# Turning pages, window keys, selected keys and probabilities as two 64-row halves in a decoder step

## The reference

```python
x_n, x_f = nsa_block(...), fox_block(...)      # both on the same projections of x
mix = (sigmoid(ga) * (x_n @ w_a) + sigmoid(gb) * (x_f @ w_b)) @ w_out
x = layer_norm(ALPHA * x + mix)
f = (gelu(conv(x @ w_up)) * (x @ w_gate)) @ w_down
x = layer_norm(ALPHA * x + f);  x = x + sigmoid(x @ w_ple_gate) * (p_emb @ w_ple)
```

## Time and profile before

| what | value |
|---|---|
| time, median of 3 runs | 2362.68 (2359.55 to 2363.3) |
| profiled execution, its own time | 2361.97 |
| its span, first to last instruction | 2360.2 |
| TensorE busy, matmuls | 2310.0 (98%) |
| VectorE, GpSimd, ScalarE busy | 1214.4, 833.7, 547.6 |
| mean granted TensorE clock | 0.998 |
| DMA moved | 240.36 MB, mean 102 GB/s |
| request stage | from 677.6 to 932.3 in the span |

### The profile page before, as it was taken

The page is one execution under the profiler, slowest core; times in us unless marked ns, Lnnn a source line. Parts: engine busy times, 40 slices in busy tenths (PEclk is TensorE's granted clock), DMA queues, the critical chain, the costliest instruction groups (busy, mean ns, idle before and its releaser), DMA issues.

```text
span 2360.2 us, 32397 instructions
## 1 busy us (share of the span) xinstructions
PE 2310.0 (98%) x11863; PEld 1518.5 (64%) x11863; DVE 1214.4 (51%) x3023; ACT 547.6 (23%) x1300; POOL 833.7 (35%) x874
## 2 busy tenths in 40 slices
PE   8999999999989998999999999999999999999999
PEld 4454566666667776788884478888888874443343
DVE  4886627787853334324225873334433334239765
ACT  0000116787753332111112121111111100001131
POOL 0000005565651002666634534333333436203531
PEclk9999999999999999999999999999999999999999
DMA  5422821031078887222226111111111126434101
GB/s 184 115 76 77 291 84 64 2 112 33 2 217 237 242 237 235 79 85 81 82 71 172 42 41 55 37 37 54 37 36 37 54 89 211 149 135 152 56 18 58
DMA packets 185959, 240.36 MB, mean 102 GB/s; under 512 B 53435, under 2 KB 128833, under 8 KB 184265
## 3 DMA queue, kind: packets, MB, share of 16 engines
q1 hardware_dynamic: 181018, 218.99, 30.2%
q0 software_dynamic: 3616, 9.73, 1.2%
q10 hardware_dynamic: 1168, 9.58, 1.2%
HBM read 216.18 MB, written 37.99 MB: 108 GB/s over the span
## 4 chain that ended last, share of the span: by engine, by line
PE 57%; DVE 2%; ACT 1%; issue 0%; DVEq 0%; ACTq 0%
PE ps L2254 37%; PE ps L2418 11%; PE ps L2307 5%; PE ps L2475 2%; PE ps L2405 1%; DVE xT L152 1%; PE ps L2483 1%; ACT xT L2528 0%; PE ps L2311 0%; DVE arena L3006 0%; ACT arena L2625 0%; DVE stats L2680 0%; PE ps L2350 0%; DVE xT L1409 0%; DVE queries L3009 0%
## 5 line engine op out<-in xcount | busy, mean ns | idle before, releaser
L2254 PE MATMUL ps<-xT,arena 128*128 128x272 f32 x1920 | 472.7, 393 | 1.8 <-DVE arena L1411 1.8
L2254 PEld LDWEIGHTS ps<-xT,arena 128*128 128x128 f32 x1920 | 363.9, 190 | 77.4 <-DVE arena L1411 2.2
L2254 PE MATMUL ps<-queries,arena 128*128 128x272 f32 x1312 | 331.6, 393 | 2.0 <-PEq L1451 1.0
L2254 PEld LDWEIGHTS ps<-queries,arena 128*128 128x128 f32 x1312 | 249.0, 190 | 54.1 <-DVE queries L2821 1.4
L235 PE MATMUL ps<-arena,xT 128*128 128x512 f32 (+1 forms) x512 | 198.3, 550 | 1.9 <-DMA arena<-in_w_in 1.1
L235 PEld LDWEIGHTS ps<-arena,xT 128*128 128x128 f32 x512 | 97.9, 192 | 101.9 <-issue 93.5
L2254 PE MATMUL ps<-arena 128*128 128x272 f32 x576 | 147.7, 393 | 0.0
L979 ACT ACTIVATE arena<-arena 128x640 f32<-128x640 f32 (+10 forms) x208 | 136.8, 660 | 33.9 <-DVE arena L929 26.1
L2418 PE MATMUL ps<-arena 128*128 128x512 f32 x312 | 140.6, 599 | 0.0
L816 PE MATMUL ps<-arena,queries 64*128 64x512 f32 (+9 forms) x704 | 132.6, 442 | 3.6 <-DVE arena L929 2.6
L2418 PE MATMUL ps<-xT,arena 128*128 128x512 f32 x304 | 131.4, 592 | 0.0
(11 more groups left out here) (357 smaller groups left out, 3411.8 us busy)
## 6 DMA issues: line engine op xcount, KB each, us to landing
arena<-in_cache_fox_kv SPq DMA_DIRECT2D x72, 256.0 KB, 4.0
arena<-in_w_ffn_down SPq DMA_DIRECT2D x68, 256.0 KB, 3.7
arena<-in_w_in SPq DMA_DIRECT2D x16, 1024.0 KB, 5.3
xT<-in_w_ffn_down SPq DMA_DIRECT2D x64, 256.0 KB, 3.6
xT<-in_cache_fox_kv SPq DMA_DIRECT2D x56, 256.0 KB, 6.3
arena<-in_cache_nsa_kv SPq DMA_DIRECT2D x64, 192.0 KB, 8.3
arena<-in_w_ffn_up SPq DMA_DIRECT2D x11, 1024.0 KB, 5.4
arena<-in_w_ffn_gate SPq DMA_DIRECT2D x11, 1024.0 KB
```

The costliest lines, as they stand in the source:

```text
L2254: mm = pe.matmul(ps[:, first + BANK_OF[z], 0:PIECE], weight[:, j, :], moving[:, j, :], start=(j == 0 and z in (1, 6, 5, 7)), stop=(j == kk ...
```

## The change

A new helper `turn_sides` turns eight tiles at once. Each 128-row tile is taken as two halves: rows 0 to 63 go through the upper half of the array into one bank and rows 64 to 127 through the lower half into another. The two banks together hold what two banks held before, but divided by row half instead of by tile. Both are entered before the first half, and both are signalled by the last one (`then_inc(ring_filled, 2)`). This takes the place of `turn` for the FoX key pages, the selected keys, the window keys, and the probabilities p_slc and p_fox. ScalarE copies the first halves of all eight tiles, VectorE the second halves, each in strips of 64 columns. The selected keys are grouped by request instead of by half of the rows, and `slc_scores` waits for all four banks before its first matmul. The raw rows, p_cmp, p_win, the new-row probabilities and the outputs are turned as before.

```diff
         if now:
-            yield from ((n, f"slc{x}{'ab'[r]}", r) for x in range(2) for r in range(2))
+            yield from ((n, f"slc{r}{'ab'[side]}", side) for r in range(2) for side in range(2))
...
+            def turn_sides(n, name_a, name_b, tiles):
+                banks = (enter(n, name_a), enter(n, name_b))
+                for x, src in enumerate(tiles):
+                    for side in range(2):
+                        rows = slice(side * HD, (side + 1) * HD)
+                        mm = pe.transpose(ps[:, banks[side], x * HD:(x + 1) * HD], src[rows], keep.ident[rows, rows])
+                mm.then_inc(ring_filled, 2)
+
             def keys(n, p):
                 pe.wait_ge(k_in[p % 4], 32 * (2 * n + p // 4 + 1))
-                for r in range(2):
-                    b = enter(n, f"k{p}{'ab'[r]}")
-                    for c in range(4):
-                        mm = turn(b, c * P, P, at.pages[:, p % 4, r, c * P:(c + 1) * P])
-                    mm.then_inc(ring_filled, 1)
+                turn_sides(n, f"k{p}a", f"k{p}b", [at.pages[:, p % 4, r, c * P:(c + 1) * P] for r in range(2) for c in range(4)])
...
             def slc_turns(n):
-                for x in range(2):
-                    for r in range(2):
-                        b = enter(n, f"slc{x}{'ab'[r]}")
-                        for j in range(4):
-                            mm = turn(b, j * P, P, at.raw[:, r, 2 * x + j // 2, j % 2, 256:384])
-                        mm.then_inc(ring_filled, 1)
+                for r in range(2):
+                    turn_sides(n, f"slc{r}a", f"slc{r}b", [at.raw[:, r, j // 2, j % 2, 256:384] for j in range(8)])
...
                 pe.wait_ge(win_in, 32 * (n + 1))
-                for r in range(2):
-                    b = enter(n, f"win{'ab'[r]}")
-                    for j in range(4):
-                        mm = turn(b, j * P, P, at.win[:, r, j, 0:P])
-                    mm.then_inc(ring_filled, 1)
+                turn_sides(n, "wina", "winb", [at.win[:, r, j, 0:P] for r in range(2) for j in range(4)])
...
+                for r in range(2):
+                    consumed(n, f"slc{r}a")
+                    consumed(n, f"slc{r}b")
                 for x in range(2):
-                    consumed(n, f"slc{x}a")
-                    consumed(n, f"slc{x}b")
...
-                    prob_turns(m, "p_slc0", at.p_slc, range(4))
-                    prob_turns(m, "p_slc1", at.p_slc, range(4, 8))
+                    turn_sides(m, "p_slc0", "p_slc1", [at.p_slc[:, j * P:(j + 1) * P] for j in range(NPAGE)])
...
-                    prob_turns(n, "p_fox0", at.p_fox, range(4))
-                    prob_turns(n, "p_fox1", at.p_fox, range(4, 8))
+                    turn_sides(n, "p_fox0", "p_fox1", [at.p_fox[:, j * P:(j + 1) * P] for j in range(NPAGE)])
...
-                        save(n, f"k{p}a", at.kT[:, p % 2, 0], tiles(ring.bank(n, f"k{p}a"), 4))
+                        save(n, f"k{p}a", at.kT[:, p % 2].rearrange("p r c q -> p (r c) q")[:, :, 0:HD], sides(ring.bank(n, f"k{p}a")))
...
-                        save(n, f"k{p}b", at.kT[:, p % 2, 1], tiles(ring.bank(n, f"k{p}b"), 4))
+                        save(n, f"k{p}b", at.kT[:, p % 2].rearrange("p r c q -> p (r c) q")[:, :, HD:P], sides(ring.bank(n, f"k{p}b")))
```

More of the change, by code:

```diff
@@ L1857, in exps, with sides @@
                                      accum_out=at.sums[:, j:j + 1]).then_inc(done, 1)
-            def tiles(b, m):
-                return ps[:, b, 0:m * P].rearrange("p (t q) -> p t q", t=m)
+            def sides(b):
+                return ps[:, b, :].rearrange("p (t q) -> p t q", t=8)
             def raw_rows(n, kv, par):
@@ L1893, in _ @@
                 if late:
-                    save(m, "p_slc0", at.pT_slc[:, 0:4, :], tiles(ring.bank(m, "p_slc0"), 4))
+                    save(m, "p_slc0", at.pT_slc[:, 0:8, 0:HD], sides(ring.bank(m, "p_slc0")))
                     save(m, "p_slc_new", at.pT_slc[0:64, 8, :], ps[0:64, ring.bank(m, "p_slc_new"), 0:P])
@@ L1903, in _ @@
                     raw_rows(n, 1, 1)
[L1904 to L1907, removed]
+                    for r in range(2):
+                        save(n, f"slc{r}a", at.slcT[:, r].rearrange("p (a q t) -> p a t q", a=4, t=2)[:, :, :, 0:HD],
+                             ps[:, ring.bank(n, f"slc{r}a"), :].rearrange("p (a t q) -> p a t q", a=4, t=2))
+                    save(n, "p_fox0", at.pT_fox[:, 0:8, 0:HD], sides(ring.bank(n, "p_fox0")))
                     save(n, "p_fox_new", at.pT_fox[0:64, 8, :], ps[0:64, ring.bank(n, "p_fox_new"), 0:P])
@@ L1910, in _ @@
                         gelu(n, kv)
-                    save(n, "wina", at.winT[:, 0, :], ps[:, ring.bank(n, "wina"), :])
+                    save(n, "wina", at.winT.rearrange("p r (j q) -> p (r j) q", q=P)[:, :, 0:HD], sides(ring.bank(n, "wina")))
                     act.wait_ge(cmp_logits, n + 1)
@@ L2014, in _ @@
                 if late:
-                    save(m, "p_slc1", at.pT_slc[:, 4:8, :], tiles(ring.bank(m, "p_slc1"), 4))
+                    save(m, "p_slc1", at.pT_slc[:, 0:8, HD:P], sides(ring.bank(m, "p_slc1")))
                 if now:
@@ L2049, in _ @@
                 if now:
-                    for x in range(2):
-                        save(n, f"slc{x}b", at.slcT[:, 1, x * 512:(x + 1) * 512].rearrange("p (a q t) -> p a t q", a=2, t=2),
-                             ps[:, ring.bank(n, f"slc{x}b"), :].rearrange("p (a t q) -> p a t q", a=2, t=2))
+                    for r in range(2):
+                        save(n, f"slc{r}b", at.slcT[:, r].rearrange("p (a q t) -> p a t q", a=4, t=2)[:, :, :, HD:P],
+                             ps[:, ring.bank(n, f"slc{r}b"), :].rearrange("p (a t q) -> p a t q", a=4, t=2))
                     dve.wait_ge(fox_exp, n + 1)
                     inverse(n, fox_inv, at.sums[:, FOX_C:FOX_C + 1], fox_inverse, 2 * n)
-                    save(n, "p_fox1", at.pT_fox[:, 4:8, :], tiles(ring.bank(n, "p_fox1"), 4))
+                    save(n, "p_fox1", at.pT_fox[:, 0:8, HD:P], sides(ring.bank(n, "p_fox1")))
                     if n < N_ - 1:
@@ L2062, in _ @@
                                           ps[:, b, 0:P].rearrange("p (r n) -> p r n", r=2)[:, :, 0:CMP_N]).then_inc(ring_dve, 1)
-                    save(n, "winb", at.winT[:, 1, :], ps[:, ring.bank(n, "winb"), :])
+                    save(n, "winb", at.winT.rearrange("p r (j q) -> p (r j) q", q=P)[:, :, HD:P], sides(ring.bank(n, "winb")))
                     if n == 0:
```

## The result

The changed kernel takes 2373.52 us (median of 5 runs, 2372.22 to 2376.63), the kernel before 2362.68 (5 runs, 2359.55 to 2363.92). The ratio is 1.0048 [1.0036, 1.006]. The change costs 10.8 us, and the result lies outside the range of the prediction. The profiled execution of after took 2376.63, its span is 2374.8, and its mean granted clock is 0.989 where before has 0.998.

What follows compares the result with a forecast made beforehand. TensorE was taken to bound rounds 1 to 3, DMA the first half of round 0. Gains of 3.6 + 0.4 + 0 = 4.0 us off 2361.97 gave 2358.0, plus 0.7 for the median: 2358.7 us, range 2345 to 2365.

Steps and rivals of the forecast that it cites:

- the saving of a pair: Turning a pair of banks in 16 halves takes 0.66 us instead of 1.02, saving 0.36 us.
- the stalls ahead of the chain: In late rounds keys(0), keys(1) and keys(4) wait for free banks; the stalls at keys(0) and keys(4) are the unsure ones.
- The walk through the round: Step through round 2 from the window pair to the raw turns: a gain of 2.17 us.
- the wake: Time from the end of a bank's copy to the next turn on TensorE: taken as 0.06 us.
- the last window pair: The window pair of round 3, counted apart from the three late rounds: another 0.36 us gained.
- Round 0: First round: 0.6 us gained ahead of the raw turns, 0.6 lost behind them; zero in sum, from -1 to +1.
- the chain of three: Two selected pairs and p_fox, nothing between, start 1.42 us apart in late rounds: loss of 0.96 us each, 0 to 1.4.
- the clock rival: Half-idle TensorE in three successive pairs drops the clock for 7 us, losing 3.5 us per late round; chance 0.10.
- The rival's own total: Kernel time if the clock fell in each late round: 3.5 us lost three times, less 4.0 gained, 2369 us; chance 0.10.
- the expected gain: Pairs from the window keys through p_slc, ahead of the raw turns, save 2.17 us in each late round.

Runs made afterwards that it cites:

- e1: The changed kernel with selected keys and p_fox turned as in the kernel before; page keys, window keys and p_slc stay in pairs: 2355.18 us, 0.9975 to before.
- e5: The changed kernel with unread identity matmuls in the chain's idle stretches, 4 before the first selected pair, 2 at three other places: 2362.52 us, 1.0001 to before.
- e7: The kernel before with full turns, but both banks of selected keys and p_fox entered first and signalled by the last turn: 2378.79 us, 1.0074 to before.
- e4: The changed kernel with p_fox and first FoX values moved ahead of the selected pairs, one hidden layer after each selected pair: 2362.03 us, 0.9998 to before.
- e6: The changed kernel reordered: hidden layer 0 after the raw turns, p_fox, first FoX values, selected pair, hidden layer 1, selected pair: 2357.19 us, 0.9976 to before.
- e3: The changed kernel with more unread identity matmuls in the chain's idle stretches, 8 before the first selected pair, 5 at three other places: 2369.14 us, 1.0033 to before.
- e8: The changed kernel with only the selected keys turned as in the kernel before; p_fox stays in a pair: 2357.63 us, 0.9982 to before.

## Why the prediction was wrong, point by point

**Right: the saving of a pair, and the stalls ahead of the chain.** 16 halves take 0.64 us to the next score matmul (684.63 less 683.99), predicted 0.66. Pages are 1.67 us apart, predicted 1.68. The walk through the round said 2.17 us up to the raw turns, window pair included; the trace shows 1.97. Counted from `win_scores`, keys(0), keys(1) and keys(4) start at 2.10, 3.68 and 11.23 us, where the walk has 2.00, 3.50 and 10.91; each stall is some 0.1 longer than worked out (see the wake below). e1, which keeps these parts alone, gained 5.9 us by its ratio (3.3 to 8.3); three times 2.17 and 0.36 for the last window pair are 6.9.

**Round 0: right in the sum, by luck.** From the first keys to `win_scores` it takes 56.8 us in both kernels, but the terms of the zero were wrong. The raw turns start 1.2 us earlier against the first keys (18.16 behind them for 19.36), where 0.6 was taken and 0.9 was the bound; the wait ahead of them grew from 2.27 to 3.06, not to 3.9. The window pair gives 0.4. The clock took it back: it falls in this chain too, and the first FoX values hold TensorE for 5.09 us (710.44 to 715.53) where they held it for 3.58. From the raw turns to the FoX values it takes as long as before (11.56 for 11.49), with a stretch at the lower clock in both.

**Too small: the chain of three, at full clock.** Predicted 0.96 a round, measured 1.46 with the filler in the gaps. In e5 the steps are 1.52, 1.53 and 1.74, where the text had 1.42, 1.42 and 1.55. The text timed a step by ScalarE's copy (0.63) and 0.06 for the wake, which gives 1.44 and not 1.42. In pass 2 the profile names VectorE's copy (0.69) as the one that ends the wait, but both end within 0.1 us of each other, and the ring asks for ScalarE's. Round 0 of after settles it for the second pair: it starts at 707.19, ScalarE's copy has ended at 707.04 and VectorE's ends at 707.44. So the copy was right, and the mis-sized term is the wake. From the end of the copy that a pair needs to its first turn it takes 0.14 to 0.16 us: here, behind VectorE's copy ahead of keys(4) (812.81 to 812.95), and with full turns in e7 (774.05 to 774.19). The text took 0.06, which a single bank shows before (807.29 to 807.35). The FoX values start 0.26 behind the last copy (710.18 to 710.44). Why a pair takes longer is not shown. FoX values also wait for the copy of p_fox_new, behind p_fox0 on ScalarE. This is 0.5 a round, and it lay inside the range of 0 to 1.4 that the text gave.

**Wrong: the step that kept the clock out of the sum.** The prediction priced the clock rival well: 3.5 us a round where 3.4 were measured, in the place it named. It gave it 0.10, because "before, no window of a late round shows less than 1.00". That was no evidence: before had no such stretch. The row that did bear on it was the other one: in round 0 a stretch with TensorE busy 0.73 of 2 us was followed by a clock of 0.56. The chain of the forecast, three pairs in 4.4 us with TensorE working half the time, comes near it. By that row the rival deserved far more than 0.10, and the clock a term in the sum, which put it at nothing. Three times 3.4 is 10 us, against a forecast gain of 4. That 3.5 came so near is in part luck: the clock was low for some 10 us and not 7, but for 2 of them TensorE stood waiting anyway.

**The rival's own total was short too.** It said 2369; 2373.5 came. Of the 4.5 between them, 1.5 is the chain's longer waits and 0.6 the smaller saving per round. The rest, 2.4, lies outside the three rounds, which are 8.8 us longer of the 10.8. The profiled execution of after, itself 3.1 above the median, reaches its first keys 3.1 later than before's (680.72 for 677.63); its clock is low from 676 to 680, ahead of the change. Another 2.7 stands behind the last `win_scores`, where the clock is low in parts of 934 to 950. Such a stretch at the start of the trunk shows in the one trace of every changed kernel, e1 too (924 to 928), and not in that of before. Whether the change brings it or chance does is open.

**What stays open.** Which pattern of idle brings the clock down: e4 and e7 show the same instructions with and without a fall. In after it fell in all four rounds, in e7 in one of the late ones, in e6 at another place, behind a single wait. In the traces with the row of waits filled or removed (e3, e5, e1, e8) no late round shows a fall. The runs say that the risk goes with the waits, and not more.

**Where the expected gain went.** It arrived (1.97 us a round) and was given back some 15 us later in the same round: 1.46 in new waits, 3.4 in the clock that these waits brought down.

## What to carry to other kernels

Before a change makes a saving by filling several buffers under one signal, count the buffers in the ring: with three banks and two to a pair, no pair is turned while the one before it is copied, unless other matmuls stand between them. Price idle time of TensorE twice, once as the wait and once as the half-speed matmuls behind it, and look in the trace for the emptiest stretch that kept its clock as well as for one that lost it. A change of one form at five places is five changes: three of them together (page keys, window keys, p_slc) made the kernel faster here (2355.2), and the other two together made it slower (2375.6).

## What the runs showed of the hardware

**Useless matmuls can pay.** Two float32 128x128 matmuls in each gap of 0.8 us, four in the first, kept the clock at 2.4 GHz and saved 11 us of 2373.5 (e5 against after).

**The clock falls on short waits.** In after, pass 2, it fell behind waits of 1.15 and 0.80 us with 16 halves between them: the next 16 halves already take 1.11 us, and the clock stays at 1.2 GHz for some 10 us. In e6 it fell behind one wait of 1.87. It needn't fall: e4 and e7 kept it through the same waits in one round and two, e6 through 1.93.

**A turn that waits for two banks starts later.** TensorE starts a pair 0.14 to 0.16 us behind the end of the copy that it needs, behind either engine and with halves or full turns (after: 707.04 to 707.19, 812.81 to 812.95; e7: 774.05 to 774.19). Before, a single bank took 0.06 (807.29 to 807.35). The cause is not shown.
